# Two-layer decoder trunk on one core: a rebuilt beginning, and values that come out with tokens on partitions

## The reference, cut to what matters

```python
for l in range(DEPTH):                                   # DEPTH = 2
    x = x + 0.5 * swiglu(rmsnorm(x, norm_ffn1_g[l]), ...)  # D_FF = 2816
    h = rmsnorm(x, norm_mix_g[l])
    proj = h @ w_in[l]                                   # q, k, v, conv b/c/u, two gates
    lam = exp(sum(lq1*lk1)) - exp(sum(lq2*lk2)) + lambda_init
    p   = softmax(q1 k1 + bias) - lam * softmax(q2 k2 + bias)   # 4 heads, T5 bias table
    attn = rmsnorm(p @ v, subln_g[l]) * (1 - lambda_init)
    y_conv = (c_b * causal_conv(c_c * c_u)) @ w_branch_conv[l]
    x = x + (sigmoid(g_attn) * (attn @ w_branch_attn[l]) + sigmoid(g_conv) * y_conv) @ w_out[l]
    x = x + 0.5 * swiglu(rmsnorm(x, norm_ffn2_g[l]), ...)
return rmsnorm(x, final_g)
```

## Time and profile before

| what | value |
|---|---|
| time, median of 3 runs | 1100.95 us (1100.90 to 1101.44) |
| time of the profiled execution | 1100.44 us |
| span of its instructions | 1098.7 us |
| PE busy | 1082.2 us, 98% |
| DVE busy | 816.4 us, 74% |
| ACT busy | 635.7 us, 58% |
| data moved | 202.18 MB, 184 GB/s in the mean |

### The profile page before, as it was taken

One profiled execution on the slowest core, in us unless ns is written; L12 is line 12 of the kernel. 1 busy time (PEld: TensorE's weight loads), 2 busy tenths in 40 slices (PEclk: granted clock), 3 DMA queues, 4 the chain that ended last, 5 costly groups with the idle time before them and its releaser, 6 DMA issues.

```text
span 1098.7 us, 19086 instructions
## 1 busy us (share of the span) xinstructions
PE 1082.2 (98%) x6404; PEld 952.9 (87%) x6404; DVE 816.4 (74%) x1004; ACT 635.7 (58%) x903; POOL 20.1 (2%) x39
## 2 busy tenths in 40 slices
PE   6999999999999999999999999999999999999997
PEld 5888888888899988888888888888888998888886
DVE  5876766878798887776787776668788988777653
ACT  7665644556675665654565555446667756655642
POOL 5100000000000000000000000000000000000000
PEclk8999999999999999999999999999999999999999
DMA  8766556655565566565566665566455655665562
GB/s 220 237 192 200 175 166 199 192 181 160 162 191 189 171 189 200 172 198 172 183 190 206 190 191 171 184 204 198 145 161 181 203 181 182 197 195 178 186 194 75
DMA packets 196420, 202.18 MB, mean 184 GB/s; under 512 B 7888, under 2 KB 189168, under 8 KB 196384
## 3 DMA queue, kind: packets, MB, share of 16 engines
q1 hardware_dynamic: 194112, 199.25, 58.8%
q0 software_dynamic: 1136, 2.40, 1.0%
q10 hardware_dynamic: 1136, 0.05, 0.1%
HBM read 199.85 MB, written 1.84 MB: 184 GB/s over the span
## 4 chain that ended last, share of the span: by engine, by line
PE 96%; DVE 1%; ACT 1%; DMA 1%; issue 0%; SPq 0%; ACTq 0%; DVEq 0%
PE acc L1232 54%; PE acc L1241 29%; PE acc L1236 4%; PE acc L1304 2%; PE acc L1305 2%; PE acc L1303 2%; DMA raw<-in_ffn_w_gate_dram 1%; PE mixed L1236 1%; PE score L1236 1%; PE score L1371 0%; PE mixed L1241 0%; PE score L1241 0%; DVE w_lo L818 0%; PE mixed L1392 0%; PE mixed L1379 0%
## 5 line engine op out<-in xcount | busy, mean ns | idle before, releaser
L1232 PE MATMUL acc<-xm,w_hi 128*128 128x512 f32 x2048 | 647.9, 398 | 3.4 <-ACT xt L637 3.1
L818 DVE TENSOR_TENSOR w_lo<-raw,w_hi 128x1024 fp32r<-128x1024 f32 x382 | 452.0, 1205 | 140.5 <-ACT w_hi L502 140.2
L1241 PEld LDWEIGHTS acc<-xm,w_lo 128*128 128x128 f32 x2048 | 385.9, 188 | 91.3
L502 ACT CAST w_hi<-raw 128x1024 fp32r<-128x1024 f32 x382 | 386.4, 1034 | 123.8 <-PE acc L1241 88.1
L1241 PE MATMUL acc<-xm,w_lo 128*128 128x256 f32 x2048 | 403.6, 278 | 0.0
L1232 PEld LDWEIGHTS acc<-xm,w_hi 128*128 128x128 f32 x2048 | 313.4, 189 | 4.2 <-ACT xt L637 3.4
L1232 PE MATMUL acc<-hm,w_hi 128*128 128x512 f32 x528 | 165.8, 395 | 0.0
L514 ACT COPY acc_lo<-acc 128x512 f32<-128x512 f32 x140 | 81.8, 584 | 123.0 <-PE acc L1241 121.8
L1241 PEld LDWEIGHTS acc<-hm,w_lo 128*128 128x128 f32 x720 | 129.1, 189 | 23.4
L1241 PE MATMUL acc<-hm,w_lo 128*128 128x256 f32 x720 | 142.4, 279 | 0.0
L830 DVE TENSOR_TENSOR sum<-acc,acc_lo 128x512 f32<-128x512 f32 x140 | 96.4, 688 | 43.6 <-ACT acc_lo L514 43.4
(11 more groups left out here) (163 smaller groups left out, 557.4 us busy)
## 6 DMA issues: line engine op xcount, KB each, us to landing
raw<-in_ffn_w_gate_dram SPq DMA_DIRECT2D x88, 512.0 KB, 4.7
raw<-in_ffn_w_up_dram SPq DMA_DIRECT2D x88, 512.0 KB, 4.0
raw<-in_ffn_w_down_dram SPq DMA_DIRECT2D x82, 512.0 KB, 4.7
raw<-in_w_in_dram SPq DMA_DIRECT2D x80, 512.0 KB, 4.4
raw<-in_w_out_dram SPq DMA_DIRECT2D x16, 512.0 KB, 4.0
raw<-in_w_branch_attn_dram SPq DMA_DIRECT2D x8, 512.0 KB, 3.6
raw<-in_w_branch_conv_dram SPq DMA_DIRECT2D x8, 512.0 KB, 3.7
raw<-in_ffn_w_down_dram SPq DMA_DIRECT2D x12, 256.0 KB, 3.2
```

The costliest lines, as they stand in the source:

```text
L502: nc.scalar.copy(w_hi[:, s, 0:tiles, :], raw[:, s, 0:tiles, :]).then_inc(hi_split, 1)
L818: nc.vector.tensor_tensor(w_lo[:, s, 0:tiles, :], raw[:, s, 0:tiles, :], w_hi[:, s, 0:tiles, :], ALU.subtract).then_inc(lo_split, 1)
L1232: nc.tensor.matmul(banks[:, m, :], w_hi[:, r, k, cols], x[:, 0:2 * SEQ], start=first and k == 0, stop=False, skip_group_check=True)
L1241: mm = nc.tensor.matmul(banks[:, m, 0:SEQ], w_lo[:, r, k, cols], x[:, 0:SEQ], start=False, stop=last and k == ends, skip_group_check=True)
```

## The change

The beginning is written anew.

- SP loads x as a first quarter, a second quarter and, after the first gate and up units, the second half.
- The gain comes as eight rows of 512 bytes, which PE turns and DVE copies to `first_g`.
- POOL makes the ones first. Eight products of the ones with themselves (`WARM`) run on PE before x is there. POOL issues the lambda rows, the parameters and the bias rows only after the third hidden pair (`hid_hi` of 3).
- x is turned into four PSUM banks and stays there for a while. ACT rounds it with its gain straight from PSUM (L696), DVE makes the low half from PSUM (L1118). The squares are also taken from PSUM (L706). The copies to `xt` come later, inside the first gate and up (L628).
- The bias table is spread with one product per head instead of two, with high and low part on 64 partitions. Two of the four bias rows are copied by DVE.
- The first unit is rounded in two halves (`hi_half`), and its high products run before its low ones (`multiply_in_two`).
- The first gate and up has its own order on ACT, DVE and PE (`first_gate_up`, `first_sets`). The mean square follows the fourth unit.
- The sums for lambda are one DVE reduction at the end of the first gate and up. The exponentials follow the Exp table in the mixer.

In the mixer, q and k are two iterations of the old form. The values are four units of 128 rows by 512 columns, two row tiles each. PE holds `xm` as the stationary operand and streams the weights, so tokens come out on partitions. ACT scales them with the root, turned to one value per token, straight into `v_tok` for all heads. `head_qkv`, its copies, the value transposes and their copies are gone; the scores read `proj`. The PE's loop over heads is written out. In every norm, `mean_sq` now precedes the clearing of `square_sum`, and the gate is scaled before `half_rstd` is made.

On ACT, at the beginning, what is there of before is this (first fence), and of the change this (second). `mixed` and `score` are the PSUM banks with x, `part` holds the bucket places, `proj` the bias rows.

The core of the diff:

```diff
@@ SP
-            for b in range(2):
-                half = slice(b * D_MODEL // 2, (b + 1) * D_MODEL // 2)
+            def load_second_half():
+                half = slice(D_MODEL // 2, D_MODEL)
                 sp.dma_start(x_tok[:, :, half],
-                             x[0].rearrange("(t p) d -> p t d", p=P)[:, :, half]).then_inc(x_loaded[b], 16)
+                             x[0].rearrange("(t p) d -> p t d", p=P)[:, :, half]).then_inc(x_loaded[1], 16)
+            for sem_at, part_at in ((x_first, slice(0, COLS)), (x_loaded[0], slice(COLS, 2 * COLS))):
+                sp.dma_start(x_tok[:, :, part_at],
+                             x[0].rearrange("(t p) d -> p t d", p=P)[:, :, part_at]).then_inc(sem_at, 16)
...
-                with loop(sp, IN_COLS // (2 * COLS), {split: 4}, 1) as i:
+                two_sets(l, w_in, 2 * COLS, w_in, 3 * COLS)
+                values(w_in, l)
+                with loop(sp, IN_COLS // (2 * COLS), {split: 4}, QKV_ITERS) as i:
@@ POOL
+            pool.wait_ge(hid_hi, 3)
             for n, v in enumerate((lambda_q1, lambda_k1, lambda_q2, lambda_k2)):
@@ ACT
+            def first_gate_up():
+                hi()
+                squares_of(2, 3)
+                hi()
+                hidden.add()
+                act.wait_ge(square_added, 3)
+                copy_acc(3)
+                for p in range(XPAIRS):
+                    nc.scalar.copy(xt[:, at(p * PAIR), :].rearrange("p k n -> p (k n)"), turned_x[p]).then_inc(x_new, 1)
+                act.wait_ge(square_added, XPAIRS)
+                copy_acc(1)
+                hi()
+                norm_root()
+                hi()
+                wait(act, (gate_ready, hidden.now))
+                nc.scalar.activation(silu[:, :, :], sums[0][:, :, :], ACT.Silu).then_inc(silu_done, 1)
...
+                    hi()
+                wait(act, (rstd_turned, layers.now + 1))
+                units_done.add(4)
+                for t, done in enumerate(((v_summed, layers.now + 1), (used, units_done.now))):
+                    wait(act, done)
+                    nc.scalar.activation(v_tok[:, t, :], acc[(sets.fixed + t) % ACCS][:, 0, :], ACT.Copy,
+                                         scale=rstd_tok[:, t:t + 1]).then_inc(acc_summed, 1)
...
-                    wait(act, (v_turned, head.now))
-                    nc.scalar.copy(v_tok[:, :, :].rearrange("p t d -> p (t d)"), v_ps).then_inc(v_copied, 1)
@@ DVE
+            def pairs_lo(first):
+                for p in (first, first + 1):
+                    dve.wait_ge(xm_hi, p + 1)
+                    for k in range(PAIR):
+                        t = p * PAIR + k
+                        last = nc.vector.scalar_tensor_tensor(
+                            out=xm[:, t, SEQ:2 * SEQ], in0=turned_x[p][:, k * SEQ:(k + 1) * SEQ],
+                            scalar=first_g[:, t:t + 1], in1=xm[:, t, 0:SEQ].bitcast(F32), op0=ALU.mult,
+                            op1=ALU.subtract)
+                    last.then_inc(xm_lo, 1)
...
+            pairs_lo(0)
+            lo()
+            lo()
+            dve.wait_ge(bias_spread, 1)
+            for h in (0, 1):
+                last = nc.vector.tensor_copy(bias_rows[:, h, :], spread[h][:, 0:BIAS_LEN])
+            last.then_inc(bias_half, 1)
+            add_square(1)
+            lo()
+            pairs_lo(2)
@@ PE
+            def first_sets():
+                halves = [[xm[:, k, :] for k in range(n, n + UK)] for n in (0, UK)]
+                gate = new_set()
+                multiply_in_two(gate, halves[0])
+                pe.wait_ge(bias_copied, 1)
+                turn_pairs(2)
+                pe.wait_ge(bias_half, 1)
+                up = new_set()
+                multiply(up, halves[0], True, False)
+                multiply(gate, halves[1], False, True, by_pair=XPAIRS // 2 + 1)
+                multiply(up, halves[1], False, True)
+                mean_square(1)
...
+            pe.wait_ge(ones_ready, 1)
+            for _ in range(WARM):
+                nc.tensor.matmul(warm_ps, mean_ones[:, :], mean_ones[:, :], start=True, stop=True)
...
+                def values():
+                    banks = [new_set()[:, 0, :], None]
+                    for u in range(KT // VK):
...
+                        for t in range(QT):
+                            if banks[t] is None:
+                                banks[t] = new_set()[:, 0, :]
+                            for k in range(VK):
...
+                                nc.tensor.matmul(banks[t], xh, wh, start=kt == 0, stop=False, skip_group_check=True)
+                                nc.tensor.matmul(banks[t], xl, wh, start=False, stop=False, skip_group_check=True)
+                                mm = nc.tensor.matmul(banks[t], xh, wl, start=False, stop=ends,
+                                                      skip_group_check=True)
+                            if ends and t == 0:
+                                mm.then_inc(v_summed, 1)
...
-                    wait(pe, (head_copied, head.now + layers.now))
...
-                    for t in range(QT):
-                        mm = nc.tensor.transpose(v_ps[:, t * V_DIM:(t + 1) * V_DIM],
-                                                 head_qkv[:, 2, t * P:(t + 1) * P], ident[:, :])
-                    mm.then_inc(v_turned, 1)
```

More of the change, by code:

```diff
@@ L358, in two_sets, with values @@
                     load(rows(wb, l)[:, k:k + UK, bass.ds(b, COLS)])
+                    if half_way and not k:
+                        half_way()
+            def values(w, l):
+                for k in range(0, KT, VK):
+                    s = slot[0] % RING
+                    wait(sp, (lo_split, split.now))
+                    sp.dma_start(raw[:, s, :, :].rearrange("p (k h) n -> p k (h n)", k=VK),
+                                 rows(w, l)[:, k:k + VK, 2 * QK_W:2 * QK_W + ATTN_W]).then_inc(loaded[s], 16)
+                    split.add()
+                    slot[0] += 1
             def last_down(w, l):
@@ L633, in _, with pairs_hi @@
-            squares = (square_sum, square, acc_lo[0], acc_lo[1])
-            for first in range(0, XPAIRS, 2):
+            act.wait_ge(ones_ready, 2)
+            have_table(ACT.Silu)
+            act.wait_ge(places_loaded, 16)
+            for n in range(2):
+                last = nc.scalar.copy(onehot_r[n * NUM_BUCKETS:(n + 1) * NUM_BUCKETS, :], onehot[0:NUM_BUCKETS, :])
+            last.then_inc(onehot_ready, 1)
+            def pairs_hi(first):
                 for p in (first, first + 1):
@@ new lines, in _ @@
+            for half, done in ((slice(0, UK // 2), hi_half), (slice(UK // 2, UK), hi_split)):
+                nc.scalar.copy(w_hi[:, 0, half, :], raw[:, 0, half, :]).then_inc(done, 1)
+            split.add()
+            slot[0] += 1
+            hi()
+            act.wait_ge(bias_spread, 1)
+            for h in (2, 3):
+                last = nc.scalar.copy(bias_rows[:, h, :], spread[h][:, 0:BIAS_LEN])
+            last.then_inc(bias_copied, 1)
+            squares_of(0, 1)
+            hi()
@@ L1219, in _, with multiply_in_two, multiply @@
             slot = [0]
-            def multiply(banks, x_tiles, first, last, *needs, halves=True):
+            def multiply_in_two(banks, x_tiles):
+                r = slot[0] % RING
+                for k, x in enumerate(x_tiles):
+                    if k % PAIR == 0:
+                        wait(pe, (xm_lo, k // PAIR + 1), (hi_split, unit.now + 1) if k else (hi_half, 1))
+                    for m in range(PAIR):
+                        nc.tensor.matmul(banks[:, m, :], w_hi[:, r, k, m * P:(m + 1) * P], x[:, 0:2 * SEQ],
+                                         start=k == 0, stop=False, skip_group_check=True)
+                wait(pe, (lo_split, unit.now + 1 + RING))
+                for k, x in enumerate(x_tiles):
+                    for m in range(PAIR):
+                        mm = nc.tensor.matmul(banks[:, m, 0:SEQ], w_lo[:, r, k, m * P:(m + 1) * P], x[:, 0:SEQ],
+                                              start=False, stop=False, skip_group_check=True)
+                mm.then_inc(used, 1)
+                unit.add()
+                slot[0] += 1
+            def multiply(banks, x_tiles, first, last, *needs, halves=True, by_pair=None):
                 r = slot[0] % RING
@@ L1228, in multiply @@
                 for k, x in enumerate(x_tiles):
+                    if by_pair and k % PAIR == 0:
+                        wait(pe, (xm_lo, by_pair + k // PAIR))
                     for m in range(PAIR):
@@ L1363, in _ @@
+                values_scaled = values()
                 first_unit()
-                with loop(pe, HEAD_ITERS, {unit: 4, sets: 2, head: 1}):
+                wait(pe, (proj_ready, 2 * V_ITER * (layers.now + 1)))
+                for h in range(HEAD_ITERS):
                     head.add()
-                    wait(pe, (head_copied, head.now + layers.now))
                     for sm in range(2):
```

(7 more changed lines are left out.)

301 lines of the change are left out of this document (171 added, 130 removed).

## The result

| | before | after |
|---|---|---|
| time, median | 1100.93 us (1100.90 to 1101.44, 4 runs) | 1093.97 us (1092.96 to 1095.37, 4 runs) |
| ratio, 95% interval | | 0.9939 (0.9927 to 0.9951) |
| profiled execution, its span | 1100.44, 1098.7 us | 1095.37, 1093.4 us |
| PE busy in the span | 98% | 99% |

The change is faster by 7.0 us; 7.5 were forecast, to 1093.4. Its runs spread by 2.4 us, those of before by 0.5. Two more series, on other chips, gave 1095.63 and 1096.19 us. Over all 14 runs of the change the median is 1095.2, the lowest 1092.83, the highest 1096.77. So one result needs two explanations: where 7 us went, and why one program takes 1093 in one execution and 1096.8 in another.

The account below looks back on a forecast made before the run. PE, busy in 98% of the span, bounds the kernel. Beginning -5.0, value transposes -2.1 and gathered heads -0.4 sum to -7.5 us on 1100.44, 1092.9; with 0.5 for the median, 1093.4, range 1090.8 to 1097.8.

Parts of the forecast that it names:

- -5.0 in the beginning: Kernel start up to the ninth gate and up unit: that unit starts earlier, counted -5.0 us, bounds -1 and -6.5.
- -2.5 in the mixer: Mixer: value transposes gone, -2.1 us, and waits for gathered heads gone, -0.4; the new values themselves 0.0.
- one of my own signs: Beginning: the forecast is wrong if the clock's rows show the lower level past 12 us.
- The table's split on DVE: Beginning, bias table: its split starts once the gain is copied, at 5.2 us, and ends at 6.3.
- Weights don't bind here: Beginning, first product with weights: two x quarters and the first unit queue 1 MB, formerly 1.5; PE starts at 8.1.
- The walk: Step-by-step timing of the beginning: first product with weights at 8.1 us, unit 4 at 20.65, unit 8 at 34.1.
- The two waits for `w_lo`: First gate and up: PE idles 1.1 us ahead of unit 6 and 1.1 us again ahead of unit 7.
- rival B: Beginning: the clock stays or falls low up to about 16 us, gaining 2.0 instead of 5.0; 1096.4 us, chance 0.24.
- A head's two value transposes: Mixer heads: removing them saves 0.26 us per head, -2.1 over 8 heads, bounds -1.6 and -3.5.
- The wait at the values' seventh product: Mixer values: the seventh product opens an accumulator the last k set just filled, a new wait of about 0.2 us.
- C: The beginning gains nothing and only the mixer's -2.5 us is left; 1098.4 us, chance 0.08.
- D: POOL's late transfers, some 50 us and later, starve PE of weights, 12.4 us of waits; 1105.8 us, chance 0.04.

Follow-up runs that it names:

- the filled execution: Changed kernel with eight more warm products behind the first eight transposes, where PE waits for the bias table; this series 1093.67 us, ratio 0.9936.
- the other bank: Changed kernel with the values' second accumulator in the scores' PSUM bank instead of the one the last k set has just filled; 1094.23 us, ratio 0.9939.
- the values alone: Kernel before, with its old beginning, given only the change's mixer (values with tokens on partitions, no value transposes); 1099.03 us against 1100.69, ratio 0.9985.
- the best version: Changed kernel with eight products filling the hole, values' second accumulator in the scores' bank, and reordered ACT and DVE work in first gate and up; 1092.70, again 1092.39 us.
- table first: Changed kernel with ACT issuing the bias table's load ahead of the gain and the places; 1096.75 us, ratio 0.9963.
- POOL's transfers: Changed kernel with POOL issuing lambda rows, parameters and bias rows at once instead of after the third hidden pair; 1097.19 us, ratio 0.9967.

## Why the prediction was right, and which steps were not

**The whole.** Forecast 1093.4, measured 1093.97. The terms add up in the profile after, but each is smaller than I put it: -3.4 for -5.0 in the beginning, -1.8 for -2.5 in the mixer. That the median is so near is in part the luck of its four runs; over 14 runs (1095.2) the forecast is 1.8 too low, and well inside the range. By one of my own signs the forecast was wrong in the profile after: the clock's rows show the lower level past 12 us, to 12.7. There the first product (9.46, for 8 to 9), unit 4 (23.29, for about 21) and unit 8 (36.61, for 34 to 36) miss what I gave for them; in the fastest execution all three hold (8.34, 20.80, 34.11).

**The beginning: two steps failed.** "The table's split on DVE starts when the gain is copied, at 5.2": it starts when the table has landed, 6.95 in the profile after, 5.67 in the fastest. I had asked of x and of the weights when they land, and not of the 0.5 KB on ACT's queue, whose landing the old beginning never waited for. The Trainium skill, "DMA: Bandwidth & Descriptors", section "Issuing engines are not separate DMA queues", says that transfers run on the same 16 DMA engines and interleave, whoever issues them. The runs agree: in the change's three profiles the table took 3.9 to 5.2 us from issue to landing beside SP's loads, and 6.8 with POOL's there too.

"Weights don't bind here" failed as well. The walk needed the first unit by 7.5, when ACT is through with x; it landed at 8.67. So the chain of waits after runs through it, and not through the table, which answers to the earlier trace rows:

```profile
1.74 6.93 DMA raw<-in_ffn_w_gate_dram
```

Behind the late table that cost PE 0.4 us; by this chain an earlier table would not have brought the first product ahead of 9.46 there. What the late table did was to leave the hole ahead of it. In the fastest execution ACT starts on the unit at 7.56 without a wait, and the step held.

**The rest of the walk held.** From unit 4 to unit 8 I had 34.1 - 20.65 = 13.45; it is 13.32 after and 13.31 in the fastest execution. The two waits for `w_lo` stand where I put them, ahead of units 6 and 7. The list gives them 1.5 us, but the starts lie 13.32 - 4 x 2.79 = 2.2 apart from a stream, my 2.2: PE's way back into the stream is lost too.

**The clock (rival B).** The forecast and B turned out not to exclude each other: they are two executions of one program. I had taken 0.9 off for landings and clock together; they cost 2.5 in the profile after, and close to nothing in the fastest. Of the 2.5, the filled execution with a table as late (unit 4 at 21.78) puts 1.5 to the clock and 1.0 to the landings. B's 1096.4 is what the five runs at 0.995 take. Of such a run of the change there is no profile; but the kernel with the other bank has the same beginning, and its profiled execution is one at 0.995, with a hole of 1.81 us ahead of 7.87. Its granted clock (columns as above):

```profile
7.00:8.00 1.00, 0.13 (x1) 0.13 (x1) 0.93 (x3) 0.57 (x2) 0.00 (x0) 0.75 1.10 399
8.00:14.00 6.00, 6.00 (x17) 4.79 (x18) 5.86 (x10) 4.97 (x8) 0.00 (x0) 0.50 1.03 336
14.00:15.00 1.00, 1.00 (x10) 1.00 (x8) 0.76 (x1) 0.00 (x0) 0.00 (x0) 0.83 0.83 254
```

The lower level lasts from about 7.5 to 14.3 there, 6.8 us instead of 3.4; unit 4 starts at 24.05 and unit 8 at 37.36, where B had 38. That the five runs are of this kind is inferred from their mean clock and time. In one thing my argument against B was wrong: I held the holes to be too short to matter, and one of 1.71 us was enough. Of the Trainium skill's rule that transposes don't bring the full clock ("TensorE: Matmul & The Clock Gate", Part 4), the runs show no more than before. Without the warm products PE ran turns alone from 4.17 to 6.57, and the clock was still low at 8.03; but a wait of 1.5 us lay between, so this doesn't tell the two readings apart.

**The mixer: the mechanism right, the size off.** A head's two value transposes were worth 0.18, not 0.26. I had read 0.20 from the starts and put 0.06 on top for the way PE's pairs are printed; the reading was the better number. Eight heads give -1.4 instead of -2.1. The waits for the gathered heads went (-0.4). The wait at the values' seventh product is there for the reason I gave, 0.28 instead of 0.2, and the other bank showed that it is this accumulator.

**C and D.** C (the beginning gains nothing) is out: with the values alone the time is 1099.0. D (POOL's late transfers starve PE) is out as well; left early, they cost 1.6 us, so the move that I counted at nothing was worth that.

## What to carry to other kernels

When waits are taken out of a beginning, list every transfer that the first product hangs on, the smallest too, and take its landing from issue to landing under the load of that moment; the one that nobody waited for before is the likeliest next wait. A hole in PE's work at the start costs what the clock loses behind it, even where another wait behind it hides the hole itself; and products that nobody needs, put *into* the hole, can be worth more than the same number ahead of it (here 1.5 us in the best version, against nothing in the median). Where a kernel's runs spread, compare its fastest with its slowest profile before any other experiment.

## What the runs showed of the hardware that was not expected

- TensorE's clock fell behind short holes: after 1.71 and 0.4 us (from about 9.2 to 12.7), and in the best version without the filling after 1.0 and 0.6 (0.50 in 10 to 11). With holes of 0.3 and 0.5, in the change's fastest profiled execution, it stayed at the upper level.
- The lower stretch lasted 3.4 us in these two profiles, and 6.8 behind 3.1 us (before), 1.81 (other bank), 1.78 (table first) and 3.9 (POOL's transfers). Whether the length of the hole or its moment decides between the two is not shown.
- As the third of three transfers on ACT's queue the 0.5 KB table landed 3.9 to 5.9 us after its issue (ten profiles without POOL's loads beside it), and 2.3 as the first; the 48 KB of places took 4.8 as the third and 3.3 to 3.7 as the second.
- The landing of 0.5 KB varied from 3.9 to 5.2 us between profiled executions of the same program, whose runs spread over 3.9 us; with the hole filled they spread over 1.0.
